# The first down projection in seven block products in place of eight, for three of its four groups

## The chip, the cores and the metric

The kernel runs on one core of one Trainium2 chip. A core has five engines that run side by side: TensorE (PE in the profile, its weight loads PEld), VectorE (DVE), ScalarE (ACT), GpSimd (POOL) and SyncE (SP), which here only starts DMAs. Each engine works through its own instructions in the order written and waits for others on semaphores. The metric is the device time of one execution in microseconds; the lower the better.

## The reference, cut to what matters

Two transformer blocks follow one another on an input of 512 tokens and 1024 features, all in float32. The change touches the feed-forward part of the first block:

```python
x = layer_norm(DEEPNORM_ALPHA * x + mix, ln1_g, ln1_b)            # 512 x 1024
h = jnp.square(jax.nn.relu(jnp.einsum("bsd,df->bsf", x, w_ff1)))  # 512 x 4096
ff = jnp.einsum("bsf,fd->bsd", h, w_ff2)                          # 512 x 1024
x = layer_norm(DEEPNORM_ALPHA * x + ff, ln2_g, ln2_b)
```

Before it stands a block of attention in two branches, after it a second block with a gated delta rule, an attention and a gated feed-forward part. None of these is touched.

## The kernel before, in words

Everything is held feature by token: a tile of 128 partitions holds 128 features, its 512 columns are the tokens. A weight matrix is cut into panels of 128 output features; a panel (`Wraw`, 128x1024) holds eight blocks of 128x128, one for each 128 input features, and is the stationary operand. Float32 products are made of two parts each, a high part (`Whi`, `Rm`, type fp32r) and the rest (`Wlo` and its like): ScalarE copies the raw tile to the high part ("split"), VectorE subtracts it from the raw tile ("low"). One block product is three matmuls of 128x128 by 128x512: low weights by high data, high by low, high by high. A panel is thus 24 matmuls into one PSUM bank (`project`, and the `mm` item of TensorE).

The feed-forward part takes up-panels (`w_ff1`) and down-panels (`w_ff2`) in groups: nine up-panels (0 to 8), eight down-panels over hidden features 0 to 7 (group 0), eight up-panels, group 1, eight, group 2, seven, group 3 (`ff_order`). So one up-panel always runs ahead of its group, except before group 3. After each up-panel comes the item `relu2`: ScalarE's ReLU out of the bank, VectorE's square, ScalarE's copy to the high part, VectorE's low part. After each down-panel comes `down`: VectorE adds the bank onto the residual tile `F(m)` in SBUF; group 0 first scales it by ALPHA in the same instruction. In group 3 sums for the layer norm follow as well.

All engines walk one list, `WORK`, made by `order_of_work`, and each does its own share of each item in that order. An instruction that has to wait therefore holds up all that stand behind it on its engine. `take` keeps four panels split ahead (`HL`) and four raw buffers loading (`RAW`); `low_weights`, called after the fourth block of a panel, puts the pending lows into the list. `Waits` leaves out a wait that a former one covers.

Of the kernel before, what the change touches and what calls it, by code (L numbers as in the profile page):

```python
# [118 lines left out]
NTH = {p: n for n, p in enumerate(PANELS)}  # L119
RAW = 4  # L120
HL = 4
# [21 lines left out]
def order_of_work():  # L143

    work, side, later = [], [], []
    st = {"loads": 0, "splits": 0, "lows": 0, "taken": 0, "done": 0}

# [19 lines left out]
    def ready_weights(upto):  # L167
        while st["splits"] < min(len(PANELS), upto) and st["splits"] - HL < st["done"]:
            while st["loads"] < min(len(PANELS), st["splits"] + RAW):
                load_weights()  # L170
            do("split", st["splits"])
            st["splits"] += 1

    def low_weights(upto=None):
# [13 lines left out]
    def project(name, i, steps=0, flush_at=3, then=None, between=(), low_at=LOW_AT):  # L188
        n = take(name, i)
        many = steps_of(name)  # L190
        do("panel", n)
        for p, k in enumerate(k_order(name)):
            do("mm", n, k)
            if p == many - 1:
                st["done"] = n + 1
            if p == flush_at:
                flush()
            for q, *item in between:
                if q == p:
# [8 lines left out]
        return n  # L208

    def project_first(names, skew=0, between=(), lows=None, apart=False):  # L210
# [223 lines left out]

    first = project_first([("w_ff1", i) for i in range(3)], apart=True)
    for kind, i in FF1:
        if kind == "up":
            n = first[i] if i < 3 else project("w_ff1", i)
            do("relu2", i)
        else:  # L440
            for m in range(8):
                n = project("w_ff2", 8 * i + m)
                do("down", n)
                if i == 3:
                    do("sum", 1, m)

# [312 lines left out]

RING_OF = {"panel": "P", "panelb": "P", "score": "S", "babank": "S", "baturn": "S", "vturn": "T", "turn": "T",  # L760
# [100 lines left out]
SUM1, SUM2, SQ, SUM1_ALL = 22, 23, 24, 27  # L861
RELU, SQUARE = 28, 31
CG, WBA, R1 = 45, 44, 38
KTM, VTM, QTM, GK, GQ = 0, 4, 8, 12, 16
# [5 lines left out]
U3, C3, R2, R3 = 24, 27, 39, 40  # L870
HID = [(2 * j, 2 * j + 1) for j in range(8)] + [(32, 33)]
HID2 = [(16 + 2 * j, 17 + 2 * j) for j in range(9)]
# [35 lines left out]
def build(nc, a, out):  # L908

    ctx = ExitStack()  # L910
    with ctx:
        def sb(name, shape, dt=F32):
            return ctx.enter_context(nc.sbuf_tensor(name, shape, dt))

        Fm = sb("Fm", [128, 49, 512])
        Rm = sb("Rm", [128, 22, 512], F32R)
# [27 lines left out]
        def G(i):  # L944
            return Xf[:, i, :]

        def bank(*item):
# [84 lines left out]


        def features(name, i, k):
            if name == "w_in":
# [9 lines left out]
            if name == "w_ff2":  # L1045
                return tuple(R(j) for j in HID[(8 * (i // 8) + k) % 9])
            if name in ("w_in_2", "w_up"):
# [5 lines left out]
        def parts_of(name, i, k):  # L1053
# [248 lines left out]
        def tensor_engine(e):  # L1302
            w = Waits(e)

            def mm(o, l, r, first=True, last=True):
                return e.matmul(o, l, r, start=first, stop=last)  # L1306

            def tr(o, x):
                return e.transpose(o, x, ident)  # L1309
# [6 lines left out]
            for what, *i in WORK:  # L1316
                if what == "mm":
# [381 lines left out]
        def scalar_engine(e):  # L1699
# [5 lines left out]
            def panel(n):  # L1705
                w.wait_ge(SG["panel"], n + 1)
                return bank("panel", n)

            for what, *i in WORK:
                if what == "split":  # L1710
                    n, = i
                    part = slice(512 if n == 0 else 0, 128 * steps_of(PANELS[n][0]))
                    w.wait_ge(SG[f"landed{n % RAW}"], 16 * (n // RAW + 1))
                    if n >= HL:
                        w.wait_ge(SG["panel"], n - HL + 1)
                    act(Whi[:, n % HL, part], Wraw[:, n % RAW, part]).then_inc(SG["w_hi"], 1)

# [137 lines left out]
                elif what == "splity":  # L1855
                    j, = i
                    w.wait_ge(SG["normed"], at("normed", 0, j))
                    act(R(16 + 2 * j), F(j), ACT.Identity, bias=col("ln1_b", j), scale=col("ln1_g", j)).then_inc(SG["y_hi"], 1)

                elif what == "relu2":  # L1860
                    j, = i
# [3 lines left out]
                    act(F(RELU + j % 3), b, ACT.Relu).then_inc(SG["relu"], 1)  # L1865
                    w.wait_ge(SG["squared"], j + 1)
                    if j >= 9:
                        w.wait_ge(SG["panel"], NTH["w_ff2", 8 * ((j - 9) // 8) + 7] + 1)
                    act(R(HID[j % 9][0]), F(SQUARE + j % 3)).then_inc(SG["hid_hi"], 1)

# [158 lines left out]
                elif what == "gated2":  # L2029
# [5 lines left out]
                    if j >= 9:  # L2035
                        w.wait_ge(SG["panel"], NTH["w_down", 8 * ((j - 9) // 8) + 7] + 1)
                    act(R(HID2[j % 9][0]), F(C3 + g % 6)).then_inc(SG["hid2_hi"], 1)
# [18 lines left out]
        def vector_engine(e):  # L2056
# [20 lines left out]
            def panel(n, item="panel"):  # L2077
                w.wait_ge(SG["panel"], n + 1)
                return bank(item, n)

            for what, *i in WORK:
                if what == "low":
                    n, = i
                    part = slice(512 if n == 0 else 0, 128 * steps_of(PANELS[n][0]))
                    w.wait_ge(SG["w_hi"], n + 1)
# [218 lines left out]
                elif what == "lowy":  # L2304
# [3 lines left out]
                    tt(R(17 + 2 * j), F(j), R(16 + 2 * j).bitcast(F32), ALU.subtract).then_inc(SG["y_lo"], 1)  # L2308

                elif what == "relu2":  # L2310
                    j, = i
                    w.wait_ge(SG["relu"], at("relu2", j))
                    if j >= 3:
                        w.wait_ge(SG["hid_hi"], j - 2)
                    f = F(SQUARE + j % 3)
                    tt(f, F(RELU + j % 3), F(RELU + j % 3), ALU.mult).then_inc(SG["squared"], 1)
                    w.wait_ge(SG["hid_hi"], j + 1)
                    hi, lo = (R(s) for s in HID[j % 9])
                    tt(lo, f, hi.bitcast(F32), ALU.subtract).then_inc(SG["hid_lo"], 1)

                elif what == "down":
                    n, = i
                    g, m = PANELS[n][1] // 8, PANELS[n][1] % 8
                    b = panel(n)
                    if g == 0:
                        w.wait_ge(SG["y_hi"], m + 1)
                        w.wait_ge(SG["y_lo"], m + 1)
                        stt(F(m), F(m), ALPHA, b, ALU.mult, ALU.add).then_inc(SG["down"], 1)
                    else:
                        w.wait_ge(SG["down"], at("down", NTH["w_ff2", 8 * g - 8 + m]))  # L2330
                        tt(F(m), F(m), b, ALU.add).then_inc(SG["down"], 1)

# [425 lines left out]
        def sync_engine(e):  # L2758
# [5 lines left out]
            for what, *i in WORK:  # L2764
                if what == "load":
# [3 lines left out]
                    if n >= RAW:  # L2769
                        w.wait_ge(SG["w_hi"], n - RAW + 1)  # L2770
                        w.wait_ge(*low_part(n - RAW))
                    if n == 0:
                        dma(SG["first_landed"], Wraw[:, 0, 0:512], a[name][j][:, 0:512])
# [40 lines left out]
                elif what == "gdnconsts":  # L2814
                    w.wait_ge(SG["gates_added"], at("merge", 7))
                    for t in range(3):
                        width = min(512, N_G * 128 - 512 * t)
# [115 lines left out]
```

## Time and profile before

| | |
|---|---|
| three runs | 1444.02 us median, 1443.52 to 1445.72 |
| the profiled execution | 1445.06 us, its span 1442.8 us |
| PE busy | 1418.2 us, 98% |
| VectorE busy | 817.0 us, 57% |
| ScalarE busy | 612.7 us, 42% |
| granted TensorE clock over the span | 1.0 |
| group 0 on TensorE | 444.04 to 487.56 us from the span's start |

The difference between the execution and its span is what lies around the first and last instruction, 2.3 us. Busy time of PE is that of overlapping matmuls: one that is recorded with 389 ns is followed by the next after less. The distance between starts is therefore what is read for the pace. VectorE and ScalarE rows too are recorded with a short tail that the next instruction overlaps.

### The profile page before, as it was taken

How to read it: one execution, taken by the hardware profiler on the slowest of the kernel's cores; microseconds unless marked ns; L12 is line 12 of the kernel's file. 1: busy time of each engine (PE TensorE's matmuls, PEld its weight loads, DVE VectorE, ACT ScalarE, POOL GpSimd, SP SyncE). 2: the span in 40 equal slices, each digit the busy share in tenths (PEclk: the TensorE clock that was granted, in tenths of full speed). 3: DMA queues.
4: the chain of work that ended last, by engine and by line, in shares of the span. 5: the costliest groups of instructions: out<-in, count | busy, mean ns of one | idle time of the engine just before them, and what ended most of it. 6: DMA issues, size and time to landing. Idle time of an engine off the chain costs nothing.

```text
span 1442.8 us, 20161 instructions
## 1 busy us (share of the span) xinstructions
PE 1418.2 (98%) x7966; PEld 1136.9 (79%) x7966; DVE 817.0 (57%) x1408; ACT 612.7 (42%) x1113; POOL 124.9 (9%) x119
## 2 busy tenths in 40 slices
PE   8999999999999999999999999999999999999998
PEld 6777777788788888888877777776778888888887
DVE  4545556656674343443468766576555673664464
ACT  4544455632362232322335755345444441442334
POOL 0000000012100000000012000440020110110012
PEclk9999999999999999999999999999999999999999
DMA  7222222123223232233223222110232332233222
GB/s 270 74 70 92 82 87 74 63 74 112 88 88 103 96 99 97 91 101 101 90 104 132 89 73 67 52 47 1 103 103 73 102 116 99 92 102 103 83 67 70
DMA packets 41501, 130.94 MB, mean 91 GB/s; under 512 B 4928, under 2 KB 7360, under 8 KB 41408
## 3 DMA queue, kind: packets, MB, share of 16 engines
q1 hardware_dynamic: 40544, 128.60, 26.5%
q8 instruction: 64, 1.05, 0.3%
q10 hardware_dynamic: 864, 1.05, 0.2%
q14 instruction: 29, 0.24, 0.1%
HBM read 124.92 MB, written 4.19 MB: 89 GB/s over the span
## 4 chain that ended last, share of the span: by engine, by line
PE 93%; DVE 3%; ACT 2%; issue 1%; DMA 1%; POOL 0%; SPq 0%; POOLq 0%; DVEq 0%; ACTq 0%
PE bank L1306 90%; PE bank L1309 3%; ACT Fm L1703 1%; DVE Fm L2061 1%; DVE Fm L2166 1%; DMA Fm<-in_x_dram 0%; DMA Fm<-in_relb_dram 0%; SPq L2762 0%; POOL Fm L2665 0%; DVE Fm L2065 0%; ACT Whi L1703 0%; POOL Xf L2665 0%; DVE sm L2065 0%; ACT Rm L1703 0%; DVE Fm L2069 0%
## 5 line engine op out<-in xcount | busy, mean ns | idle before, releaser
L1306 PE MATMUL bank<-Rm,Whi 128*128 128x512 f32 (+1 forms) x2840 | 874.5, 389 | 9.3 <-ACT Whi L1703 6.0
L1306 PEld LDWEIGHTS bank<-Rm,Whi 128*128 128x128 f32 x2840 | 532.8, 188 | 120.7 <-ACT Whi L1703 6.0
L1306 PE MATMUL bank<-Rm,Wlo 128*128 128x512 f32 (+1 forms) x1420 | 565.4, 398 | 2.0 <-issue 1.8
L2061 DVE TENSOR_TENSOR Wlo<-Wraw,Whi 128x1024 fp32r<-128x1024 f32 (+2 forms) x225 | 283.8, 1265 | 112.5 <-ACT Whi L1703 111.8
L1306 PEld LDWEIGHTS bank<-Rm,Wlo 128*128 128x128 f32 x1420 | 267.6, 188 | 61.4 <-issue 7.5
L1703 ACT ACTIVATE Whi<-Wraw 128x1024 fp32r<-128x1024 f32 (+2 forms) x225 | 232.5, 1038 | 187.1 <-PE bank L1306 181.3
L1306 PE MATMUL bank<-Xr,Whi 128*128 128x512 f32 (+1 forms) x760 | 228.4, 382 | 0.0
L2665 POOL TENSOR_TENSOR Fm<-Fm 128x512 f32<-128x512 f32 (+1 forms) x89 | 102.4, 1157 | 780.0 <-ACT Fm L1703 489.2
L1703 ACT ACTIVATE Fm<-bank 128x512 f32<-128x512 f32 (+4 forms) x200 | 92.4, 482 | 170.7 <-PE bank L1306 106.0
L1306 PEld LDWEIGHTS bank<-Xr,Whi 128*128 128x128 f32 x760 | 141.1, 188 | 27.9
L1306 PE MATMUL bank<-Xr,Wlo 128*128 128x512 f32 (+1 forms) x380 | 145.6, 383 | 0.0
L2061 DVE TENSOR_TENSOR Fm<-Fm,bank 128x512 f32<-128x512 f32 (+2 forms) x130 | 77.7, 621 | 118.0 <-PE bank L1306 117.8
L1703 ACT ACTIVATE Fm<-Fm 128x512 f32<-128x512 f32 (+2 forms) x119 | 61.5, 518 | 96.6 <-DVE Fm L2061 61.3
L1306 PE MATMUL bank<-Fm 128*64 128x128 f32 (+8 forms) x872 | 95.1, 323 | 4.3 <-ACT Fm L1703 1.9
L1703 ACT ACTIVATE Fm<-Fm,par 128x512 f32<-128x512 f32 (+1 forms) x68 | 48.1, 710 | 110.2 <-DVE Fm L2061 110.2
L2061 DVE TENSOR_TENSOR Fm<-Fm 128x512 f32<-128x512 f32 x78 | 53.5, 695 | 61.0 <-ACT Fm L1703 54.6
L1703 ACT ACTIVATE Fm<-Fm,sm 128x512 f32<-128x512 f32 (+3 forms) x93 | 53.5, 578 | 79.1 <-DVE sm L2065 66.4
L1306 PEld LDWEIGHTS bank<-Fm 128*64 128x64 f32 (+4 forms) x872 | 59.2, 155 | 34.5 <-issue 25.3
L1306 PEld LDWEIGHTS bank<-Xr,Wlo 128*128 128x128 f32 x380 | 71.4, 188 | 13.8
L2061 DVE TENSOR_TENSOR Rm<-Fm,Rm 128x512 fp32r<-128x512 f32 x57 | 38.9, 689 | 52.8 <-ACT Rm L1703 52.3
L2069 DVE SCALAR_TENSOR_TENSOR Fm<-Fm,par 128x511 f32<-128x511 f32 x88 | 65.4, 746 | 1.7 <-ACT Fm L1703 0.2
L1703 ACT ACTIVATE Rm<-Fm 128x512 fp32r<-128x512 f32 x54 | 33.7, 631 | 71.1 <-POOL Fm L2665 44.5
(100 smaller groups left out, 716.3 us busy)
## 6 DMA issues: line engine op xcount, KB each, us to landing
Wraw<-in_w_in_dram SPq DMA_DIRECT2D x67, 512.0 KB, 3.3
Wraw<-in_w_ff_dram SPq DMA_DIRECT2D x64, 512.0 KB, 3.2
Wraw<-in_w_up_dram SPq DMA_DIRECT2D x44, 512.0 KB, 3.2
Wraw<-in_w_o_dram SPq DMA_DIRECT2D x16, 512.0 KB, 3.3
Wraw<-in_w_down_dram SPq DMA_DIRECT2D x16, 512.0 KB, 3.2
Wraw<-in_w_ab_dram SPq DMA_DIRECT2D x8, 512.0 KB, 3.2
Wraw<-in_w_down_end_dram SPq DMA_DIRECT2D x8, 384.0 KB, 3.0
Fm<-in_relb_dram SPq DMA_DIRECT2D x8, 256.0 KB, 5.9
```

The source lines that it names most:

```text
L1306: return e.matmul(o, l, r, start=first, stop=last)
L1309: return e.transpose(o, x, ident)
L1703: return e.activation(o, x, func, **kw)
L2061: return e.tensor_tensor(o, x, y, op)
L2069: return e.scalar_tensor_tensor(out=o, in0=x, scalar=s, in1=y, op0=op0, op1=op1)
L2166: e.tensor_tensor_reduce(p, bank("score", u, j)[:, 0:n], strip[:, 512 - n:512], 1.0, LOW, ALU.add, ALU.max, mx).then_inc(SG["masked"], 1)
L2665: return e.tensor_tensor(o, x, y, op)
```

## The change

For groups 0 to 2 the down-panels are taken in pairs n, n+1. A pair, over 1024 hidden features and 512 tokens, is a product of two by two blocks: the stationary side has the halves of panel n (`a11`, `a12`) and of panel n+1 (`a21`, `a22`), each four 128x128 blocks; the moving side has the two halves of the hidden features (even and odd tiles, the weights are reordered to suit on the host, `halves`) by the two halves of the tokens. Seven products of such blocks, with sums of blocks as operands, replace eight. Each `product` is 4 x 3 matmuls of 128x128 by 128x256.

- VectorE sums on the weight side, for each pair (`blocks`): half 0 is `a21 + a22`, then that less `a11`, the second waiting for the first; half 1 is two more. Each is 128x512. ScalarE's `blocksplit` (128x1024) and VectorE's `blocklow` (128x1024) turn each half into high and low part. Panel n+1 is split itself in its second half only.
- On the hidden side (`hidden`), for each two tiles: VectorE makes a sum of 128x512 and two of 128x256, each waiting for the one before, ScalarE makes four high parts (one 128x256, three 128x512) and VectorE four low parts. They replace the two high and two low parts of `relu2`.
- Six `fold` additions of VectorE take the place of two `down` additions: products 1, 5, 6, 3 by 128x256, the bank of 2 and 4 by 128x512, and product 7, which goes to both halves of `F(m+1)`, by 128x512. Product 6 adds onto the bank after fold 1 has read it, 3 after fold 5, 7 after fold 6.
- Banks: a pair uses three (`total`, `single`, `fifth`), the ring P has six.
- The scaling by ALPHA is a ScalarE instruction after each of the first eight up-panels.
- The square (and ReLU) of up-panels 8, 16 and 24 is moved from behind that up-panel to behind fold 5 of the first pair.
- Group 3 stays by panels, its blocks in the order 0, 2, 4, 6, 1, 3, 5, 7. SyncE's load of a panel waits for the block sums of the panel whose buffer it takes, and its load of constants for the second block (`gdnconsts`) waits for the last down-panel.

TensorE's order in each pair is 1, 2, 5, 6, 4, 3, 7; products 5 and 6 need half 0 of the weight sums, 3 and 7 half 1.

```diff
@@ project
             if p == low_at:
                 low_weights()
+                if n + 1 in PAIRS:
+                    sum_parts(2 * st["pairs"] + 1)
...
+    def block_sums(upto):
+        while st["sums"] < min(upto, st["ready"]):
+            do("blocks", PAIRS[st["sums"] // 2], st["sums"] % 2)
+            st["sums"] += 1
+
+    def sum_parts(upto):
+        block_sums(upto)
+        while st["parts"] < min(upto, st["sums"]):
+            do("blocksplit", PAIRS[st["parts"] // 2], st["parts"] % 2)
+            do("blocklow", PAIRS[st["parts"] // 2], st["parts"] % 2)
+            st["parts"] += 1
...
+    def first_seven(name, i, then):
...
+        low_weights(st["taken"])
+        do("product", n, 1)
+        do("fold", n, 1)
+        sum_parts(2 * r + 1)
+        do("product", n, 2)
+        do("product", n, 5)
+        do("fold", n, 5)
+        do(*then)
+        sum_parts(2 * r + 2)
+        do("product", n, 6)
+        do("fold", n, 6)
+        low_weights(st["taken"] + 1)
+        do("product", n, 4)
+        do("fold", n, 4)
+        do("product", n, 3)
+        do("fold", n, 3)
+        low_weights()
+        sum_parts(2 * r + 3)
+        do("product", n, 7)
+        do("fold", n, 7)
+        block_sums(2 * r + 4)
...
+    def seven_products(name, i):
...
+        sum_parts(2 * r + 1)
+        do("product", n, 1)
+        sum_parts(2 * r + 2)
+        low_weights(st["taken"] + 1)
+        do("fold", n, 1)
+        do("product", n, 2)
+        low_weights()
+        block_sums(2 * r + 3)
+        do("product", n, 5)
+        do("fold", n, 5)
+        block_sums(2 * r + 4)
+        do("product", n, 6)
+        do("fold", n, 6)
+        sum_parts(2 * r + 3)
+        do("product", n, 4)
+        do("fold", n, 4)
+        do("product", n, 3)
+        do("fold", n, 3)
+        do("product", n, 7)
+        do("fold", n, 7)
...
     for kind, i in FF1:
         if kind == "up":
             n = first[i] if i < 3 else project("w_ff1", i)
-            do("relu2", i)
+            if i not in (8, 16, 24):
+                do("relu2", i)
+            if i % 2 and i < 24:
+                do("hidden", i // 2)
+            if i < 8:
+                do("alpha", i)
+        elif i < 3:
+            first_seven("w_ff2", 8 * i, ("relu2", 8 * i + 8))
+            for m in range(2, 8, 2):
+                seven_products("w_ff2", 8 * i + m)
...
@@ tensor_engine
+                elif what == "product":
...
+                    for k in range(4):
+                        q = 4 * g + k
+                        w.wait_ge(SG["hid_hi"], moving_made(q, p))
+                        w.wait_ge(SG["hid_lo"], moving_made(q, p))
+                        xh, xl = moving(q, p)
+                        s = slice(128 * k, 128 * k + 128)
+                        add(o, lo[:, s], xh, p in (1, 2, 5) and k == 0)
+                        add(o, hi[:, s], xl)
+                        m = add(o, hi[:, s], xh, False, k == 3)
+                    m.then_inc(SG["product"], 1)
```

## Rows read from the trace of the kernel before

**Rows 1.** The page: busy time and share of each engine, and the chain by engine.
```profile
PE 1418.2 (98%) x7966; PEld 1136.9 (79%) x7966; DVE 817.0 (57%) x1408; ACT 612.7 (42%) x1113; POOL 124.9 (9%) x119
...
PE 93%; DVE 3%; ACT 2%; issue 1%; DMA 1%; POOL 0%; SPq 0%; POOLq 0%; DVEq 0%; ACTq 0%
```

**Rows 2.** Windows on groups 0 to 2: length, each engine's busy us, clock, DMA.
```profile
444.04:487.56 43.52, 43.52 (x193) 36.04 (x192) 15.99 (x17) 9.61 (x10) 0.00 (x0) 1.00 0.33 108
531.00:574.60 43.60, 43.60 (x194) 36.08 (x193) 15.99 (x17) 9.60 (x10) 0.00 (x0) 1.00 0.33 109
618.00:661.60 43.60, 43.60 (x194) 36.12 (x193) 15.99 (x17) 9.60 (x10) 0.00 (x0) 1.00 0.33 109
```

**Rows 3.** Timeline of PE, 512-column matmuls: start, us, engine, line, operation.
```profile
438.15 0.61 PE L1306 MATMUL bank<-Xr,Whi 128*128 128x512 f32 x2
438.60 0.39 PE L1306 MATMUL bank<-Rm,Wlo 128*128 128x512 f32 x1
```

**Rows 4.** Timeline of PE in the last stage, 256-column matmuls; then a window there.
```profile
1418.63 0.28 PE L1306 MATMUL bank<-Rm,Wlo 128*128 128x256 f32 x1
1418.75 0.40 PE L1306 MATMUL bank<-Rm,Whi 128*128 128x256 f32 x2
1418.99 0.28 PE L1306 MATMUL bank<-Rm,Wlo 128*128 128x256 f32 x1
...
1416.00:1428.00 12.00, 12.00 (x103) 12.00 (x102) 4.30 (x9) 9.39 (x21) 6.39 (x7) 1.00 0.00 1
```

**Rows 5.** Timeline of ACT and DVE beside one up-panel, 438 to 443 us.
```profile
438.80 0.60 ACT L1703 ACTIVATE Fm<-bank 128x512 f32<-128x512 f32 x1 [2.50 <-PE bank L1306]
440.16 0.63 ACT L1703 ACTIVATE Rm<-Fm 128x512 fp32r<-128x512 f32 x1 [0.76 <-DVE Fm L2061]
440.69 1.04 ACT L1703 ACTIVATE Whi<-Wraw 128x1024 fp32r<-128x1024 f32 x1
...
439.43 0.69 DVE L2061 TENSOR_TENSOR Fm<-Fm 128x512 f32<-128x512 f32 x1 [1.88 <-ACT Fm L1703]
440.82 0.69 DVE L2061 TENSOR_TENSOR Rm<-Fm,Rm 128x512 fp32r<-128x512 f32 x1 [0.70 <-ACT Rm L1703]
441.77 1.22 DVE L2061 TENSOR_TENSOR Wlo<-Wraw,Whi 128x1024 fp32r<-128x1024 f32 x1 [0.26 <-ACT Whi L1703]
```

**Rows 6.** Timeline of DVE where instructions follow one another without a wait.
```profile
424.37 1.23 DVE L2061 TENSOR_TENSOR Wlo<-Wraw,Whi 128x1024 fp32r<-128x1024 f32 x1 [0.26 <-ACT Whi L1703]
425.51 0.68 DVE L2061 TENSOR_TENSOR Fm<-Fm 128x512 f32<-128x512 f32 x1
...
749.39 2.48 DVE L2061 TENSOR_TENSOR Fm<-Fm,bank 128x512 f32<-128x512 f32 x4 [0.38 <-PE bank L1306]
...
1105.24 0.69 DVE L2061 TENSOR_TENSOR Rm<-Fm,Rm 128x512 fp32r<-128x512 f32 x1 [4.27 <-ACT Rm L1703]
1105.85 1.22 DVE L2061 TENSOR_TENSOR Wlo<-Wraw,Whi 128x1024 fp32r<-128x1024 f32 x1
...
1421.53 0.74 DVE L2061 TENSOR_TENSOR Fm<-Fm,bank 128x256 f32<-128x256 f32 x2
```

**Rows 7.** Timeline of DVE: one instruction that waits for the one before it.
```profile
746.28 0.15 DVE L2279 COPY sm<-bank 128x4 f32<-128x4 f32 x1
746.47 0.16 DVE L2061 TENSOR_TENSOR sm<-sm 128x4 f32<-128x4 f32 x1
```

**Rows 8.** Timeline: a DVE instruction, and the weight load that waited for it.
```profile
761.06 1.67 DVE L2069 SCALAR_TENSOR_TENSOR Rm<-Fm,par,Rm 128x512 fp32r<-128x512 f32 x1
...
762.79 0.53 PEld L1306 LDWEIGHTS bank<-Rm,Whi 128*128 128x128 f32 x3 [0.62 <-DVE Rm L2069]
```

**Rows 9.** Timeline of PE at the kernel's start, and a window there.
```profile
5.99 0.79 PE L1306 MATMUL bank<-Rm,Whi 128*128 128x512 f32 x1 [5.99 <-ACT Whi L1703]
...
8.24 1.05 PE L1306 MATMUL bank<-Rm,Whi 128*128 128x512 f32 x2
...
9.52 1.05 PE L1306 MATMUL bank<-Rm,Whi 128*128 128x512 f32 x2
...
11.65 0.45 PE L1306 MATMUL bank<-Rm,Wlo 128*128 128x512 f32 x1
...
5.00:10.00 5.00, 4.00 (x9) 2.84 (x10) 4.30 (x7) 4.34 (x8) 0.00 (x0) 1.00 1.04 400
```

**Rows 10.** Waits of PE over the whole span: us in total, times, longest.
```profile
PE bank L1306 <- ACT Fm L1703: 2.5, 5, 0.7
...
PE bank L1306 <- DVE Fm L2061: 1.4, 2, 1.2
```

**Rows 11.** Timeline of SP after the last loads of the stage.
```profile
736.83 1.37 SPq L2762 DMA_DIRECT2D Fm<-in_cg_dram  x3
...
752.35 14.68 SPq L2762 DMA_DIRECT2D x_scratch<-Fm  x7
```

More of the change, by code:

```diff
@@ L119, with doubled, pair_of, product_end @@
 NTH = {p: n for n, p in enumerate(PANELS)}
+def doubled(n):
+    name, i = PANELS[n]
+    return name == "w_ff2" and i < 24
+PAIRS = [n for n, (_, i) in enumerate(PANELS) if doubled(n) and i % 2 == 0]
+PAIR_NO = {n: r for r, n in enumerate(PAIRS)}
+def pair_of(n):
+    return n - PANELS[n][1] % 2 if doubled(n) else None
+PRODUCTS = (1, 2, 5, 6, 4, 3, 7)
+def product_end(n, p):
+    return 7 * PAIR_NO[n] + PRODUCTS.index(p) + 1
+HALF_ORDER = (0, 2, 4, 6, 1, 3, 5, 7)
 RAW = 4
@@ L145, in order_of_work @@
     work, side, later = [], [], []
-    st = {"loads": 0, "splits": 0, "lows": 0, "taken": 0, "done": 0}
+    st = {"loads": 0, "splits": 0, "lows": 0, "taken": 0, "done": 0, "sums": 0, "ready": 0, "parts": 0, "pairs": 0}
     def do(*item):
@@ L208, in project @@
         return n
+    def first_seven(name, i, then):
+        n = take(name, i)
+        take(name, i + 1)
+        r = st["pairs"]
+        for bank in ("total", "single", "fifth"):
+            do(bank, n)
+        low_weights(st["taken"])
[19 more added lines that the diff above has]
+        block_sums(2 * r + 4)
+        st["pairs"] += 1
+        st["done"] = n + 2
+    def seven_products(name, i):
+        n = take(name, i)
+        take(name, i + 1)
+        r = st["pairs"]
+        for bank in ("total", "single", "fifth"):
+            do(bank, n)
+        sum_parts(2 * r + 1)
[18 more added lines that the diff above has]
+        do("fold", n, 7)
+        st["pairs"] += 1
+        st["done"] = n + 2
     def project_first(names, skew=0, between=(), lows=None, apart=False):
@@ L1084, in low_part, with finished @@
             return SG["w_lo"], at("low", n)
+        def finished(n):
+            if pair_of(n) is not None:
+                return SG["product"], product_end(pair_of(n), 2 if pair_of(n) == n else 4)
+            return SG["panel"], n + 1 - sum(2 for m in PAIRS if m < n)
         def emptied(n):
@@ L1129, in let_go @@
             kind, i = item[0], item[1:]
+            if kind in ("total", "single", "fifth"):
+                return [(SG["fold"], fold_end(*i, {"total": 7, "single": 4, "fifth": 3}[kind]))]
             if kind == "panel":
@@ L1306, in mm, with add @@
                 return e.matmul(o, l, r, start=first, stop=last)
+            def add(o, l, r, first=False, last=False):
+                return e.matmul(o, l, r, start=first, stop=last, skip_group_check=True)
             def tr(o, x):
@@ L1858, in scalar_engine @@
                     act(R(16 + 2 * j), F(j), ACT.Identity, bias=col("ln1_b", j), scale=col("ln1_g", j)).then_inc(SG["y_hi"], 1)
+                elif what == "blocksplit":
+                    n, half_ = i
+                    r = PAIR_NO[n]
+                    w.wait_ge(SG["blocks"], 4 * r + 2 * half_ + 2)
+                    if r > 0:
+                        w.wait_ge(SG["product"], product_end(PAIRS[r - 1], 7 if half_ else 6))
+                    hi, _, raw = combined(half_)
+                    act(hi, raw).then_inc(SG["block_hi"], 1)
                 elif what == "relu2":
@@ L2083, in vector_engine @@
                     n, = i
[L2084 removed]
+                    part = slice(512 if n == 0 or pair_of(n) == n - 1 else 0, 128 * steps_of(PANELS[n][0]))
                     w.wait_ge(SG["w_hi"], n + 1)
@@ L2771, in sync_engine @@
                         w.wait_ge(*low_part(n - RAW))
+                        if pair_of(n - RAW) is not None:
+                            w.wait_ge(SG["blocks"], 4 * PAIR_NO[pair_of(n - RAW)] + 4)
                     if n == 0:
```

209 lines of the change are left out of this document (174 added, 35 removed).

## The prediction, before the changed kernel was run

> **What bounds the kernel now.** I read the page first: PE is busy for 98% of the span and makes 93% of the chain that ended last [rows 1]; the reader is to see that nothing else bounds the whole. Then the windows on the three groups that change: PE is busy for all of each 43.5 us, VectorE for 16.0, ScalarE for 9.6, GpSimd for nothing [rows 2]. So a matmul saved is time saved, as long as the others keep up, and VectorE has 27.5 us to spare in a group. Last the timelines, for the pace of each kind of instruction and for what one takes to release another.
>
> **What TensorE saves.** With 512 columns a block product (three matmuls) starts each 0.68 us: the Xr matmuls at 438.15 and the next Wlo matmul at 438.60 are 0.45 apart, for two, and the third is as long [rows 3]; eight blocks make 5.44 us, a group of eight panels 43.52. With 256 columns three start each 0.36 us (1418.63 to 1418.99), weight loads included, at clock 1.00 [rows 4]. So a product of 4 x 3 matmuls takes 1.44 us, seven take 10.08, where two panels took 10.88: 0.80 us saved a pair, 9.6 in twelve. The ratio is 0.93 and not 7/8, as the halved matmul takes 0.12 and not 0.113. The Trainium skill, "TensorE: Matmul & The Clock Gate", section "Back-to-back issue gap", gives an isolated gap of N/2.4 plus 2.5 ns: 109 ns at 256 columns and 216 at 512, by which 48 of the one less 84 of the other would save 1.19 us a pair, an estimate of 14 in all; the trace disagrees with 120 and 227 ns, and is what I go by.
>
> **What VectorE gets.** Steps between starts where nothing waits: 1.14 us for 128x1024, 0.61 for 128x512 (1105.24 to 1105.85), 0.60 out of a bank (2.48 less 0.68, over three), 0.33 for 128x256 out of a bank (0.74 less 0.41) [rows 6]. In a pair it had two lows and two additions, 3.5 us. Now: three of 1024 columns (low of panel n, two `blocklow`), five of 512 (four sums, the half low of panel n+1), folds of 4 x 0.33 and 2 x 0.60: 3.42 + 3.05 + 2.52 = 9.0 us, against TensorE's 10.08. It fits, but barely, so the order and the handovers decide. Handovers: matmul pace to consumer 0.20 us (panel ends at 438.60, ReLU at 438.80), ScalarE to VectorE and back 0.03 (ReLU ends 439.40, square 439.43) [rows 3, 5]; an own result 0.04 after the recorded end [rows 7]; VectorE to weight load 0.06 [rows 8]. A handover counts the full recorded duration: 0.69 for 512 columns, 1.23 for 1024, ScalarE 1.05 for 1024, 0.60 for the ReLU.
>
> **The queue, walked.** T = 0 is the end of up-panel 8, when product 1 of a group's first pair can start. Without waits its product 5 is due at 2.88, product 3 at 7.20.
>
> *Stall A, before product 5.* Up-panel 7 ends at -5.44. ReLU -5.24 to -4.64, square to -3.92, sum of 512 -3.88 to -3.19, the two dependent ones of 256 start at -3.15 and -2.69, four lows at -2.36, -2.03, -1.42 and -0.81. Only then the weight low of up-panel 8's turn: it waits for a split that stands behind ALPHA on ScalarE, and starts at -0.07. First weight sum 1.07, the dependent one 1.80 to 2.49, ScalarE 2.53 to 3.58, `blocklow` 3.61 to 4.84, product 5 at 4.90: 2.02 us late. In groups 1 and 2, without ALPHA, 1.89.
>
> *Stall B, before product 3.* Product 5 ends at 6.34, fold 5 starts 6.54, the moved square 6.87, two sums 7.48 and 8.09 to 8.78, ScalarE to 9.87, `blocklow` 9.90 to 11.13, product 3 at 11.19. Products 6 and 4 ended at 9.22: 1.97 us late. In group 2 the moved item also makes the high and low part of tile 24, a handover (0.03 + 0.63 + 0.03) and a low: 1.39 more, 3.36.
>
> *Stall C, second pair.* Product 3 ends at 12.63, 7 at 14.07. Fold 3 12.83, half low 13.16, sums 13.77 and 14.50 to 15.19, ScalarE to 16.28, `blocklow` 16.31 to 17.54, product 5 at 17.60, due at 16.95: 0.65.
>
> *Stall D, second pair.* VectorE is behind now: fold 7 of the first pair 17.45, sums 18.05 and 18.66 to 19.35, ScalarE 19.39 to 20.44, `blocklow` 20.47, weight low 21.61, and only then fold 1, 22.75 to 23.17, though product 1 had ended at 15.51. Product 6 adds onto that bank, so it starts at 23.23 instead of 19.04: 4.19 us.
>
> Pairs three and four run at 10.08: in the third, fold 1 comes just before its product 6. Sum by group: stalls 8.83, 8.70 and 10.09 us, 27.6 together, against 9.6 saved: **18.0 us slower**. Some 9 us of VectorE work in a group stood within its former slack, but in the first two pairs it comes too late.
>
> Bounds. The walk's weak points are VectorE's pace on these operands and the own-result handover; neither sum nor fold with a broadcast bank stands in the trace as such. With all VectorE durations 10% shorter (it then gains 0.06 us on each sum, as if a 512 sum went at 0.55), the same walk gives +12.3; 10% longer, +23.9. With an own result at 0.10 and TensorE's restart at 0.19, a whole recorded weight load, +20.1. I take the rows as they stand, since form and size are theirs.
>
> **Costed at nothing.** ALPHA and the split hidden parts on ScalarE: 0.5 us and 0.4 more a panel where it worked 2.3 of 5.44 [rows 5]; cover gone, they push back the split, which is the 0.13 in stall A. The hidden lows in the up-panels: VectorE then works 6.9 of 10.88 us for two panels, by the steps above. Half a split saved on ScalarE. The loads' new wait: in the second pair the sums end at 19.35, a load lands some 4 later, and that panel's split is due near 29. Behind it on SP stand only more loads. The constants are issued at 736.83 and would now follow the last panel, 6.4 us later; behind them stand the spill stores, 752.35 [rows 11], and they land before. ALPHA leaving the addition, the new order of blocks in group 3: the same lengths; tile 30 is wanted fourth, 2.0 us in, but its parts were made beside up-panel 31.
>
> **Against the runs.** The trace's execution took 1445.06 us, its span 1442.8; the median of the runs is 1.0 lower. The difference goes onto the median: 1444.0 + 18.0 = 1462.
>
> **Rivals.**
> 1. *VectorE keeps up; faster.* All its work hides, TensorE takes 9.6 us less: 1434.4. For it: 9.0 us of work in 10.08, 27.5 us of slack in a group [rows 2]. Against: the slack is of the group, the stalls are of its first two pairs, and each is a chain of named instructions. It decides where stalls in a group fall below 3.2 us; a fifth less on each VectorE duration would not do that, only another order on its queue than I read. 0.12.
> 2. *Half of it.* Stall D does not come, because pair one's tail is shorter than walked (fold 7 and the sums of the next pair reach ScalarE sooner), the rest does: 27.6 - 12.6 - 9.6 = +5.4, 1449. 0.08.
> 3. *The clock falls too.* At the start, after 5.99 us of nothing, matmuls run 0.43 apart (8.24 to 9.52 for three), the 1.2 GHz pace, until about 11.65, though the column shows 1.00 [rows 9]. The longest later wait of PE is 1.2 us [rows 10], so no row tells what 4.19 do. If it fell, 256 columns take 0.213 in place of 0.12 over 5.6 us: 2.4 lost, of which 0.6 is taken up before product 7; 1.8 to 2.4 for each of three D stalls: +24, 1468. The Trainium skill, "TensorE: Matmul & The Clock Gate", section "Why this matters for your kernels", warns of idle gaps in TensorE that send it back to half rate. 0.15.
>
> My own case has 0.65. The range holds it with its bounds, rival 3 and most of rival 2: 1449 to 1471. Outside are rival 1 and the far tails, near 0.18. By 0.2%, 2.9 us, which is about what a measurement of this kernel can tell from no change: faster 0.13, within 0.03, slower 0.84.
>
> **What would show it.** PE starts 0.12 apart in products and 10.08 us for pairs three and four of a group. In the first pair a PE wait near 2 us on VectorE before product 5 and before product 3, in the second one near 4 before product 6, released by a 128x256 addition. VectorE near 100% busy over the second pair, and ScalarE's 1024-column parts starting right behind VectorE's sums. PE busy down by the saving, its waits up by some 28 us. I am wrong if the second pairs show no wait over 1 us, if three 256-column matmuls take other than 0.36, or if the waits stand in the up-panels.

## The result, and the profile after

The changed kernel takes 1475.57 us in the median of six runs (1471.43 to 1476.77), the one before 1443.94 beside it: the ratio is 1.0212, with an interval from 1.0201 to 1.0223. It is 31.6 us slower where 18.0 were forecast, and outside the range of 1449 to 1471.

The page of the changed kernel: span, busy time by engine, the chain by engine and by line. L1488 is the matmul of a `product`, L1485 that of a panel, L2299 VectorE's two-input operations, L1914 ScalarE's.

```profile
span 1474.5 us, 21350 instructions
PE 1425.6 (97%) x8398; PEld 1163.3 (79%) x8398; DVE 910.1 (62%) x1588; ACT 646.6 (44%) x1169; POOL 124.3 (8%) x119
...
PE 89%; DVE 5%; ACT 3%; issue 2%; POOL 0%; DMA 0%; POOLq 0%; DVEq 0%; ACTq 0%
PE bank L1485 79%; PE bank L1488 7%; PE bank L1491 3%; DVE Fm L2299 3%; ACT Fm L1914 1%; ACT Er L1914 1%; DVE Wlo L2299 1%; DVE Fm L2404 0%; DMA Fm<-in_x_dram 0%; DVE Er L2299 0%; ACT Whi L1914 0%; POOL Fm L2970 0%; POOL Xf L2970 0%; ACT Rm L1914 0%; DVE Fm L2303 0%
```

PE makes 89% of the chain where it made 93% [rows 1]; VectorE has 5% for 3, ScalarE 3% for 2, and time without a releaser 2% for 1. Its windows, by stage (length, busy us of PE, PEld, DVE, ACT and POOL, granted clock, DMA share, GB/s): the three groups, what follows to the layer norm, on to the second block's reload, and the rest.

```profile
443.37:495.38 52.01, 44.21 (x337) 43.44 (x337) 38.01 (x56) 16.54 (x18) 0.00 (x0) 0.93 0.29 102
538.90:590.72 51.82, 44.24 (x338) 43.48 (x337) 37.85 (x56) 16.54 (x18) 0.00 (x0) 0.93 0.30 102
634.24:688.84 54.60, 46.29 (x338) 45.70 (x337) 38.74 (x57) 17.17 (x19) 0.00 (x0) 0.87 0.28 97
688.84:770.60 81.76, 81.76 (x364) 67.73 (x363) 40.28 (x44) 26.33 (x35) 8.39 (x7) 1.00 0.29 97
770.60:1055.60 285.00, 274.13 (x2610) 206.85 (x2609) 200.51 (x421) 151.33 (x371) 45.38 (x46) 0.99 0.19 65
1055.60:1474.50 418.90, 412.32 (x1910) 343.86 (x1910) 235.55 (x312) 156.87 (x221) 45.79 (x39) 1.00 0.29 96
```

Beside [rows 2] a group is 52.0, 51.8 and 54.6 us long instead of 43.5: 27.9 more in all. VectorE works 38 us in one instead of 16. PE is idle for 8 us of each, and the clock column, 1.00 before, has 0.93 and 0.87. Outside the groups one stretch is longer, 285.0 against 280.7 us; it is called the later stretch below. The other two are as they were (81.8 and 418.9, before 81.6 and 418.9).

The waits of PE in groups, in the timeline of group 0 (start, us, engine, line, operation, what it waited for). Product 1 starts at 443.41.

```profile
448.31 0.95 PE L1488 MATMUL bank<-Rm,Er 128*128 128x256 f32 x6 [1.87 <-issue]
454.69 2.19 PE L1488 MATMUL bank<-Rm,Er 128*128 128x256 f32 x9 [1.84 <-issue]
462.35 0.95 PE L1488 MATMUL bank<-Rm,Er 128*128 128x256 f32 x6 [0.19 <-issue]
467.92 1.27 PE L1488 MATMUL bank<-Rm,Er 128*128 128x256 f32 x6 [3.90 <-DVE Fm L2299]
```

These are the four places of the walk: products 5 and 3 of the first pair, 5 and 6 of the second. The profile names VectorE for the last alone and puts the others down to issue. For the first two the times show the same engine: the weight load comes 0.06 us after the end of a `blocklow`.

```profile
446.99 1.23 DVE L2299 TENSOR_TENSOR Er<-Fm,Er 128x1024 fp32r<-128x1024 f32 x1 [1.12 <-ACT Er L1914]
448.28 0.77 PEld L1488 LDWEIGHTS bank<-Rm,Er 128*128 128x128 f32 x6 [2.04 <-issue]
...
453.36 1.23 DVE L2299 TENSOR_TENSOR Er<-Fm,Er 128x1024 fp32r<-128x1024 f32 x1 [1.13 <-ACT Er L1914]
454.65 0.86 PEld L1488 LDWEIGHTS bank<-Rm,Er 128*128 128x128 f32 x4 [2.01 <-issue]
```

VectorE's timeline before the last wait:

```profile
461.03 1.23 DVE L2299 TENSOR_TENSOR Er<-Fm,Er 128x1024 fp32r<-128x1024 f32 x1 [1.12 <-ACT Er L1914]
462.17 0.68 DVE L2299 TENSOR_TENSOR Fm<-Fm,bank 128x512 f32<-128x512 f32 x1
462.77 0.69 DVE L2299 TENSOR_TENSOR Fm<-Wraw 128x512 f32<-128x512 f32 x1
463.37 0.69 DVE L2299 TENSOR_TENSOR Fm<-Wraw,Fm 128x512 f32<-128x512 f32 x1
465.18 1.22 DVE L2299 TENSOR_TENSOR Er<-Fm,Er 128x1024 fp32r<-128x1024 f32 x1 [1.12 <-ACT Er L1914]
466.32 1.22 DVE L2299 TENSOR_TENSOR Wlo<-Wraw,Whi 128x1024 fp32r<-128x1024 f32 x1
467.46 0.41 DVE L2299 TENSOR_TENSOR Fm<-Fm,bank 128x256 f32<-128x256 f32 x1
```

Fold 7, two sums, a handover to ScalarE and back, `blocklow`, a low, and then the 0.41 us of fold 1 for which PE stands at 467.46. Last the clock, in windows of 2 us over that group (columns as above):

```profile
452.00:454.00 2.00, 0.85 (x8) 0.64 (x6) 0.87 (x2) 1.06 (x1) 0.00 (x0) 1.00 0.35 94
454.00:456.00 2.00, 1.31 (x6) 1.34 (x7) 1.51 (x3) 0.00 (x0) 0.00 (x0) 0.69 1.00 399
456.00:458.00 2.00, 2.00 (x12) 2.00 (x11) 0.45 (x2) 0.00 (x0) 0.00 (x0) 0.50 0.11 39
458.00:460.00 2.00, 2.00 (x18) 2.00 (x18) 1.87 (x3) 0.06 (x1) 0.00 (x0) 0.96 0.00 0
...
466.00:468.00 2.00, 0.08 (x1) 0.08 (x1) 2.00 (x4) 0.00 (x0) 0.00 (x0) 1.00 0.99 389
468.00:470.00 2.00, 2.00 (x11) 2.00 (x12) 1.97 (x4) 0.00 (x0) 0.00 (x0) 0.60 0.02 8
470.00:472.00 2.00, 2.00 (x12) 2.00 (x11) 2.00 (x5) 1.43 (x2) 0.00 (x0) 0.54 0.02 4
472.00:474.00 2.00, 2.00 (x19) 2.00 (x18) 1.48 (x2) 1.21 (x2) 0.00 (x0) 1.00 0.77 244
```

The reader is to see PE's busy time and the clock (the third figure from the end) together: PE idles, starts again, and then the clock falls to 0.50, which is 1.2 GHz of 2.4; 12 matmuls in 2 us where 18 or 19 run as the clock comes back. In group 2 it falls about 1 us before the wait of 3.23 us is over:

```profile
644.00:645.90 1.90, 0.00 (x0) 0.00 (x0) 0.78 (x2) 1.06 (x1) 0.00 (x0) 1.00 0.24 37
645.90:646.90 1.00, 0.00 (x1) 0.03 (x1) 1.00 (x2) 0.00 (x0) 0.00 (x0) 0.51 0.92 360
646.90:650.00 3.10, 3.10 (x14) 3.10 (x15) 0.99 (x3) 0.00 (x0) 0.00 (x0) 0.50 0.49 200
```

### The profile page after: what moved, and what is told of

Same layout as the page of the kernel before. It is cut to its first block, busy times and chain, and to the rows that moved or that the text cites. A ratio compares the mean times of both kernels' runs of the same rounds, so it can differ in the third digit from the quotient of the medians.

```text
span 1474.5 us, 21350 instructions
## 1 busy us (share of the span) xinstructions
PE 1425.6 (97%) x8398; PEld 1163.3 (79%) x8398; DVE 910.1 (62%) x1588; ACT 646.6 (44%) x1169; POOL 124.3 (8%) x119
## 3 DMA queue, kind: packets, MB, share of 16 engines
HBM read 124.92 MB, written 4.19 MB: 88 GB/s over the span
## 4 chain that ended last, share of the span: by engine, by line
PE 89%; DVE 5%; ACT 3%; issue 2%; POOL 0%; DMA 0%; POOLq 0%; DVEq 0%; ACTq 0%
PE bank L1485 79%; PE bank L1488 7%; PE bank L1491 3%; DVE Fm L2299 3%; ACT Fm L1914 1%; ACT Er L1914 1%; DVE Wlo L2299 1%; DVE Fm L2404 0%; DMA Fm<-in_x_dram 0%; DVE Er L2299 0%; ACT Whi L1914 0%; POOL Fm L2970 0%; POOL Xf L2970 0%; ACT Rm L1914 0%; DVE Fm L2303 0%
## 5 line engine op out<-in xcount | busy, mean ns | idle before, releaser
L1485 PE MATMUL bank<-Rm,Whi 128*128 128x512 f32 (+1 forms) x2488 | 766.6, 389 | 10.3 <-ACT Whi L1914 5.8
L1485 PEld LDWEIGHTS bank<-Rm,Whi 128*128 128x128 f32 x2488 | 467.1, 189 | 107.5 <-issue 5.9
L1485 PE MATMUL bank<-Rm,Wlo 128*128 128x512 f32 (+1 forms) x1244 | 497.5, 400 | 1.1 <-issue 0.9
L2299 DVE TENSOR_TENSOR Wlo<-Wraw,Whi 128x1024 fp32r<-128x1024 f32 (+2 forms) x225 | 277.5, 1238 | 96.4 <-ACT Whi L1914 95.5
L1485 PEld LDWEIGHTS bank<-Rm,Wlo 128*128 128x128 f32 x1244 | 234.7, 189 | 54.6 <-issue 7.5
L1914 ACT ACTIVATE Whi<-Wraw 128x1024 fp32r<-128x1024 f32 (+2 forms) x225 | 226.5, 1014 | 103.3 <-PE bank L1485 81.6
L1485 PE MATMUL bank<-Xr,Whi 128*128 128x512 f32 (+1 forms) x712 | 213.7, 382 | 0.0
L1914 ACT ACTIVATE Fm<-bank 128x512 f32<-128x512 f32 (+4 forms) x200 | 92.3, 482 | 171.0 <-PE bank L1485 105.3
L2299 DVE TENSOR_TENSOR Fm<-Fm,bank 128x256 f32<-128x256 f32 (+2 forms) x186 | 102.7, 571 | 100.8 <-PE bank L1485 73.8
L1485 PEld LDWEIGHTS bank<-Xr,Whi 128*128 128x128 f32 x712 | 132.1, 188 | 25.8
L1485 PE MATMUL bank<-Xr,Wlo 128*128 128x512 f32 (+1 forms) x356 | 136.3, 383 | 0.0
L1914 ACT ACTIVATE Fm<-Fm 128x512 f32<-128x512 f32 (+2 forms) x127 | 66.4, 524 | 96.0 <-DVE Fm L2299 61.3
L2299 DVE TENSOR_TENSOR Fm<-Fm 128x512 f32<-128x512 f32 (+1 forms) x114 | 71.9, 638 | 53.3 <-ACT Fm L1914 45.7
L1485 PE MATMUL bank<-Fm 128*64 128x128 f32 (+8 forms) x872 | 95.6, 324 | 3.1 <-DVE Fm L2299 1.2
L1914 ACT ACTIVATE Fm<-Fm,par 128x512 f32<-128x512 f32 (+1 forms) x68 | 48.1, 710 | 110.2 <-DVE Fm L2299 110.2
L1914 ACT ACTIVATE Fm<-Fm,sm 128x512 f32<-128x512 f32 (+3 forms) x93 | 53.5, 578 | 77.8 <-DVE sm L2303 65.1
L1485 PEld LDWEIGHTS bank<-Fm 128*64 128x64 f32 (+4 forms) x872 | 59.2, 155 | 33.6 <-issue 25.4
L1485 PEld LDWEIGHTS bank<-Xr,Wlo 128*128 128x128 f32 x356 | 66.9, 188 | 13.0
L1914 ACT ACTIVATE Er<-Fm 128x1024 fp32r<-128x1024 f32 (+2 forms) x43 | 36.1, 840 | 92.2 <-DVE Fm L2299 64.2
L1488 PE MATMUL bank<-Rm,Er 128*128 128x256 f32 x324 | 53.1, 308 | 23.7 <-issue 12.5
L1488 PEld LDWEIGHTS bank<-Rm,Er 128*128 128x128 f32 x324 | 47.4, 213 | 25.7 <-issue 13.9
```

Source lines behind the costliest of these rows:

```text
L1488: return e.matmul(o, l, r, start=first, stop=last, skip_group_check=True)
L1914: return e.activation(o, x, func, **kw)
L2299: return e.tensor_tensor(o, x, y, op)
```

## The experiments

Theory Q+C: VectorE's queue makes TensorE wait where the walk says (Q), and TensorE's clock falls after such waits (C). Rivals: P, the products themselves bring the clock down; V, VectorE has too much work wherever it stands. Each set of the e-runs ran beside the kernel before, at 1444.5 to 1444.9 us.

**e1: the waits filled.** The new item issues matmuls on operands already there into an unread bank.

```diff
+        do("spare", n, 2, 14)
         do("product", n, 5)
...
+        do("spare", n, 4, 14)
         do("product", n, 3)
... (seven_products)
+        if i % 8 == 2:
+            do("spare", n, 5, 32)
         do("product", n, 6)
```

> The changed kernel with spare matmuls on TensorE in the four places where it stood waiting: 14 of 128x256 before product 5 and 14 before product 3 of a group's first pair, 32 before product 6 of the second, on operands that are already there, into a bank nobody reads. They last less (1.7, 1.7 and 3.8 us) than the waits of 2.0, 2.0 and 4.1 us. Theory Q+C (queue and clock): VectorE comes as late as before, so the 18 us of waits less the saving stay, but TensorE's clock does not fall; 1444 + 18 = 1462, granted clock 1.00 in the three groups. Rival P (the half-rate stretches come from the products themselves, as more weight loads for each column, and not from standing still): they stay, 1475 or more. Rival V (VectorE is later than I walked and the clock column is only a symptom): within 2 us of 1475.6.

1465.11 us (1464.55 to 1467.78), ratio 1.0143 (1.0128 to 1.0158). The windows of its groups:

```profile
443.50:492.90 49.40, 48.44 (x397) 47.68 (x397) 37.85 (x56) 16.44 (x18) 0.00 (x0) 1.00 0.31 107
536.40:585.70 49.30, 48.48 (x398) 47.71 (x397) 37.78 (x56) 16.44 (x18) 0.00 (x0) 1.00 0.30 108
629.20:679.90 50.70, 48.47 (x398) 47.70 (x397) 38.48 (x57) 17.07 (x19) 0.00 (x0) 1.00 0.31 105
```

Clock 1.00 with more matmuls than ever in the stage: P falls; in the groups the standing still was the cause. 149.3 us in three groups, against 130.6 before: the queue alone costs 18.8, where the walk gave 18.0. The clock's share is 158.4 less 149.3, 9.1 us in the traces' groups. The medians are 10.5 apart, but the later stretch differs too, 283.0 us in e1's trace against 285.0. That stretch, 2.3 us longer than before, is the largest part of why the whole came out at 1465 and not 1462; the queue's 0.8 us and the kernel before, 0.9 us slower beside this set, add to it.

**e2: stall B alone.** `sum_parts(2 * r + 2)` in `first_seven` moved from behind the square to behind fold 1.

> One move: in a group's first pair the second half of the weight sums with its split and low stands behind fold 1 in place of behind fold 5 and the moved square. Theory Q+C: stall B goes (2.0, 2.0 and 3.4 us, of which 0.8 comes back in group 2 before product 7), so 6.3 us less of waiting, and the half-rate stretch that follows stall B in each group goes too, up to 1.7 us for each 3.4 us of it: 1464 to 1468. Stall D stays with its half-rate stretches. Rival Q alone (the clock falls by D alone): 1469.3. Rival P: 1469 to 1471 with as many half-rate stretches as in the changed kernel.

1466.17 us (1463.94 to 1467.81), ratio 1.0146 (1.0131 to 1.0161), as Q+C has it; no wait stands before product 3 any more, those before products 5 and 6 stay (1.87 and 3.91 us in group 0).

**e3: fold 1 first.**

```diff
         do("product", n, 1)
+        do("fold", n, 1)
         sum_parts(2 * r + 2)
         low_weights(st["taken"] + 1)
-        do("fold", n, 1)
```

> One move: in pairs two to four of a group fold 1 stands right behind product 1, ahead of the low of the second half and the next panel's low. Theory Q+C: stall D before product 6 shrinks from 4.2 to 0.7 us, but product 3 now waits 2.6 for the second half's low, so only 0.8 us a group goes, 2.5 in all; the single wait of 4 us goes too and with it perhaps one half-rate stretch a group: 1468 to 1473. Who thinks that the order of that one addition is the whole cost of stall D expects 4.2 us a group less, 1463.

1465.05 us (1461.75 to 1466.36), ratio 1.0142 (1.0125 to 1.0159): better than I expected of it, though the queue does as walked. PE's waits in the second pair are 0.42 before product 6 and 2.37 before product 3, instead of one of 3.90. In the traces the three groups take 9.3 us less than the changed kernel's 158.4. The queue accounts for 2.5 of them by the walk; the other 6.8 go with the clock, which is 0.97, 1.00 and 0.97 by group in place of 0.93, 0.93 and 0.87. The medians are 10.5 apart, but e3's later stretch is also 5.8 us shorter than the changed kernel's. One wait here, the 3.23 us before product 3 of group 2, left the clock at 1.00; in the changed kernel the clock fell in the same wait.

**e9 and e10: the spare matmuls in halves**, before the long wait alone, and before the short ones alone.

> The changed kernel with the 32 spare matmuls before product 6 of the second pair alone. All spare ones together kept the clock and brought 10.5 us. If what I now hold is right, that half-rate stretches follow the waits of 2 us as well as those of 4, this brings about half: those behind the long waits (three stretches, 3.4 to 6.8 us, at most half of each lost, less 0.6 us of slack), 4 to 6 us: 1470. The view of my prediction, that only the long waits let the clock fall, gives all of it: 1465.

> The other half: 14 spare matmuls before product 5 and 14 before product 3 of a group's first pair, none before the long wait. By what I now hold the stretches behind product 3 go and those behind the long wait stay: 4 to 6 us less than the changed kernel, 1470. If only the long waits counted: 1475.6, no change.

e9 took 1465.46 us (ratio 1.0147, 1.0133 to 1.0160), e10 1473.31 (1.0198, 1.0182 to 1.0214). My expectation of an even split was wrong: most of the clock's cost follows the waits of 3.9 us. In the traces e9's three groups take 151.2 us, e10's 155.6, with all filled 149.3: 6.3 us for three long waits left open, 1.8 for six short ones. At each of the eleven waits of 3.9 us (two in the changed kernel, three each in e2, e7 and e10) the clock fell, at the earliest 1.6 us before the wait's end and at the latest 1.3 after it. Behind the short ones it fell in some groups and not in others: 0.97 and 1.00 in e9's groups 0 and 1, whose waits were alike (1.87 and 1.84, 1.75 and 1.84). What decides for a wait of 2 or 3 us stays open.

**e7: the moved square put back.** `relu2` for 8, 16 and 24 behind their own up-panel.

> The changed kernel with the ReLU and square of up-panels 8, 16 and 24 back behind their up-panel. The queue gives 2.7 us less waiting: stall B falls from 2.0 to 1.4 in two groups and from 3.4 to 1.9 in the third, as the square no longer stands between fold 5 and the sums. Theory Q+C: 1472.9, and perhaps a half-rate stretch fewer, down to 1469. Who holds the move for a gain expects over 1477.

1470.44 us (1466.97 to 1472.64), ratio 1.0176 (1.0161 to 1.0192). So this part of the change costs 5 us by itself. In the traces 3.4 of them lie in the groups (155.0 us), where the waits before product 3 are 1.24, 0.71 and 0.65 in place of 1.84, 1.84 and 3.23; 1.8 lie in the later stretch (283.2 us), which the square doesn't touch. The clock gained nothing: 0.93, 0.90 and 0.90 by group, for 0.93, 0.93 and 0.87.

**e4: the same work, earlier and even.** In `project`, and `first_seven` in the order of `seven_products`, with the square behind fold 5:

```diff
-                if n + 1 in PAIRS:
+                if n + 2 in PAIRS:
                     sum_parts(2 * st["pairs"] + 1)
+                if n + 1 in PAIRS:
+                    sum_parts(2 * st["pairs"] + 2)
```

> The weight sums of a group's first pair start one up-panel earlier (half 0 beside up-panel 7, half 1 beside up-panel 8) and the first pair uses the even order of the later pairs: next pair's sums behind products 2 and 5 in place of the end. The work is the same. Theory Q+C: VectorE has room there; waits left are 0.8 us before product 6 and 0.1 before 7, 1.5 in group 2, 3.9 in all against 9.6 saved, and no clock falls in the groups: 1444 - 5.7 = 1438.3. Rival P (half rate by the products themselves): ten us more, 1448. Rival V (VectorE has too much work wherever it stands, 9 of 10 us a pair): waits of 1 us or more in every pair, 1448 to 1460.

1442.10 us (1438.10 to 1443.78), ratio 0.9979 (0.9970 to 0.9988). Its groups:

```profile
443.50:485.25 41.75, 40.65 (x337) 40.38 (x336) 35.52 (x54) 15.80 (x18) 0.00 (x0) 1.00 0.38 127
528.80:569.90 41.10, 40.62 (x337) 40.36 (x336) 34.94 (x53) 15.39 (x17) 0.00 (x0) 1.00 0.36 129
613.40:655.90 42.50, 40.82 (x338) 40.37 (x337) 35.68 (x54) 15.90 (x18) 0.00 (x0) 1.00 0.37 125
```

125.4 us, 5.2 less than before, where the walk had 5.7. V falls: VectorE is busy for 35 of 42 us and still hardly anyone waits. All that the change lost in the groups, waits and clock, it lost by the order in which VectorE was asked. The median is 3.8 us above the walk, and not by these groups; 0.9 of it is the kernel before, slower beside this set. **e8** has the square behind fold 6, and is otherwise the same.

> The early and even order of the fourth experiment with the moved square behind fold 6. The walk gives 0.4 us less waiting than there: 1441.7 against its 1442.1, so the same within the noise. It is here for a second look at the same schedule: whether the three groups again take some 125.4 us with granted clock 1.00, and where, if anywhere, the clock falls after them.

1442.14 us, ratio 0.9977 (0.9967 to 0.9987), groups 41.7, 41.1 and 42.4.

**e5 and e6: the weight sums on GpSimd**, in the order of the change (e5) and of e4 (e6, and e11 once more): the `blocks` item moved from `vector_engine` to `pool_engine`.

> The changed kernel with the four weight sums of each pair on GpSimd, which does nothing in this stage, in place of VectorE; order of the list as it was. VectorE's share of a pair falls from 9.0 to 6.6 us, and the sums no longer stand behind folds. Theory Q+C: by the same walk only 1.3 us of waiting are left (product 3 in group 2), so 1444.9 - 8.3 = 1436.6 if the two engines do not slow each other; in the trace of the kernel before both took longer side by side (a low of 1024 columns 1.48 to 2.05 us in place of 1.23), and with VectorE a fifth slower I get waits of 5 to 10 us: 1437 to 1446. Who holds that TensorE itself is the cause (half rate by 256-column products) expects over 1455; who holds that the loads or the banks are late expects no change from 1475.6.

> The early and even order of the fourth experiment, with the weight sums on GpSimd. The walk has no wait left, 1444.9 - 9.6 = 1435.3; with the slowing of VectorE beside GpSimd 1436 to 1441. If the 3.8 us by which the fourth experiment's median missed its walk come from later stages and not from the three groups, they show here too: 1439.

> The kernel of the sixth experiment once more, against the one before in more rounds: 1438 to 1441, ratio 0.995 to 0.998, and the three groups in 123.5 us again; the spread of its runs from places after them.

e5: 1447.72 us, ratio 1.0029 (1.0019 to 1.0039), 28 us better than the change, 1.7 outside my range. The waits in its groups are 6.6 us, inside the 5 to 10 that I took for the two engines slowing each other. What I had left out is the clock, which fell behind two waits of 1.85 us (0.96 in groups 0 and 2), and the later stretch, 283.2 us. e6: 1439.83, ratio 0.9969 (0.9955 to 0.9982); e11: 1441.00, 0.9971 (0.9962 to 0.9979). These are the fastest of all; e4 and e8 too are faster than the kernel before, by 0.2%. Groups of e6, and its GpSimd and VectorE in the second of them by form:

```profile
443.00:485.85 42.85, 40.80 (x337) 40.38 (x337) 34.12 (x45) 18.01 (x21) 17.14 (x11) 1.00 0.28 101
529.40:569.70 40.30, 40.30 (x337) 40.26 (x337) 30.03 (x40) 14.88 (x17) 16.02 (x10) 1.00 0.31 106
613.20:653.50 40.30, 40.30 (x337) 40.26 (x336) 30.65 (x41) 15.46 (x18) 16.03 (x10) 1.00 0.31 105
```

```profile
L2953 POOL TENSOR_TENSOR Fm<-Wraw 128x512 f32<-128x512 f32 x5 | 8.3, 1663 | 14.8 <-DVE Er L2301 14.8
...
L2301 DVE TENSOR_TENSOR Wlo<-Wraw,Whi 128x1024 fp32r<-128x1024 f32 x5 | 6.1, 1220 | 0.0
L2301 DVE TENSOR_TENSOR Wlo<-Wraw,Whi 128x512 fp32r<-128x512 f32 x3 | 4.6, 1528 | 0.0
```

Two groups run at 40.3 us, four times the 10.08 of the forecast: TensorE waits for nothing. VectorE's half low takes 1.53 us beside GpSimd, 0.69 without.

**b1 to b7: the untouched stretch.** From the layer norm to the reload (the later stretch) the twelve traces of changed kernels have 279.3 to 286.3 us, 283.2 in the median; only one trace of the kernel before was there. Four more of it:

> The kernel before, unchanged. If the untouched stretch from the layer norm to the reload varies by itself, four looks at it spread over some 279 to 286 us, as the eleven variants did, around 283. If its lengthening belongs to the change, they stay at 280 to 281.

> As for the first look at the kernel before: 279 to 286 us in the untouched stretch if it varies by itself, 280 to 281 if the change lengthens it.

> As for the first look at the kernel before: 279 to 286 us in the untouched stretch if it varies by itself, 280 to 281 if the change lengthens it.

> As for the first look at the kernel before: 279 to 286 us in the untouched stretch if it varies by itself, 280 to 281 if the change lengthens it.

280.9, 280.3, 280.4 and 280.1 us. So the lengthening belongs to the changed kernels, though no instruction of the stretch is another, and in them it varies from run to run: e6 and e11 are one kernel, with 281.4 and 286.3 us. In each trace of the kernel before TensorE waits there once for 0.63 to 0.90 us for nothing the profile shows, at the same matmul; in e4's trace it does not, and in e8's, whose stretch takes 285.8, it does so twice, elsewhere:

```profile
939.53 0.63 PE L1487 MATMUL bank<-Rm,Whi 128*128 128x512 f32 x2 [2.37 <-issue]
957.67 0.34 PE L1487 MATMUL bank<-Xf,Fm 64*64 64x64 f32 x5 [2.12 <-issue]
```

The next three put spare matmuls of 128x256 into the down-panels of the kernel before, behind the first block of each: 18 each for b5 and b6, 9 for b7.

> The kernel before with 18 spare matmuls of 128x256 in each down-panel of groups 0 to 2, 432 in all, as many as the change adds, into a bank nobody reads; some 52 us longer for it. If the number of TensorE instructions ahead moves its waits for nothing in the later stretch, that stretch leaves 280.1 to 280.9 us, to 282 to 286, with issue waits over 1.5 us. If only what the change does to the other engines or to its tiles matters, it stays at 280 to 281 with one issue wait of 0.6.

> The same once more: with the number of instructions as the cause 279 to 286 us in the untouched stretch, another value than in the first look being no surprise; without it 280 to 281.

> Half as many spare matmuls, 9 in each of the 24 down-panels, some 26 us longer. With the number of instructions as the cause the later stretch leaves 280 to 281 us too, and its issue waits stand at yet other places; without it 280 to 281.

279.9, 281.6 and 282.1 us, with waits for nothing at other matmuls than before: 0.69 in b5, 0.68 and 0.38 in b6, 1.82 in b7. The number of TensorE instructions ahead moves these waits, but not by as much as 432 of them come with in the changed kernels (up to 286.3). The cause of their size stays open.

The waits are not all of it: the clock falls in this stretch too. In the trace of the changed kernel it falls to 0.50 at 775.6 and at 1038.5 us, in e11 behind both waits for nothing, and once each in e2, e7, e8 and e10; of the five traces of the kernel before in b1 alone. Two lines for the changed kernel:

```profile
776.00:779.00 3.00, 3.00 (x9) 1.54 (x8) 1.82 (x4) 0.76 (x2) 0.00 (x0) 0.50 0.00 1
1039.00:1041.00 2.00, 2.00 (x7) 1.42 (x7) 1.62 (x7) 1.18 (x4) 0.00 (x0) 0.50 0.00 0
```

PE is busy there for 274.1 us in place of 270.9, though its matmuls are the same, and idle for 10.9 in place of 9.8. So some 3.3 us of what the stretch grew by in this trace are matmuls at half rate, and 1 us is waiting.

## Why the prediction was wrong, step by step

- **The saving.** Right. Three 256-column matmuls start each 0.36 us, and e6 shows four pairs in 40.30.
- **The walk.** Right in place and size. In group 0 product 5 started 4.90 us after product 1 (forecast 4.90), product 3 at 11.28 (11.19), and the wait before product 6 was 3.90 by the profile, 4.1 from its turn (4.19). Before the second pair's product 5 it was 0.19, not 0.65: product 3 had run at half clock and come late itself. Group 2's wait before product 3 was 3.23 by the profile, 3.46 from its turn (3.36), the moved item's share as forecast. With the clock held the queue costs 18.8 us (18.0). Two of its signs did not come as told: the profile names VectorE for the long wait alone, and PE's busy time went up by 7.4 us (1418.2 to 1425.6) and not down by the saving, as matmuls at half rate last longer.
- **The failed step: "My own case has 0.65"**, with the clock standing through waits of 4 us. I had no row for such a wait but one, 5.99 us at the start with the pace halved behind it [rows 9], and held the absence of a row between 1.2 and 6 us for a reason to let it stand. The near end of a gap in the rows was taken, where the far end was the only one that spoke. The Trainium skill, "TensorE: Matmul & The Clock Gate", section "Why this matters for your kernels", warned of just this; the trace agrees, with 0.50 at every wait of 3.9 us. It should have been the likeliest case. In the groups the fall of the clock cost 9.1 us (e1), the largest part of the 13.6 by which the forecast missed.
- **Rival 3** named it, but at 6 us. Three long waits cost 6.3 in the traces, 2.1 each, inside its 1.8 to 2.4. It had nothing for the short waits and for both together (9.1 in all in the traces' groups), nor for the later stretch.
- **The later stretch.** Costed at nothing without a word, as nothing in it changes. It took 4.4 us more in this trace, some 2.5 in the median of twelve, by waits for nothing and by the clock; what sets them off there is not shown. Groups 18.8 + 9.1, stretch 4.4, less 0.7 that lies ahead of group 0: 31.6.
- **Rivals 1 and 2.** Stall D came, and e4 shows what rival 1 asked for: another order on VectorE's queue.
- **Things at nothing.** The constants' later load and the loads' new wait left no trace: no wait of PE on a DMA or a split in the groups. ALPHA shows as forecast in stall A, 1.87 us in group 0 against 1.75 in the others (0.13 forecast).

## What to carry to other kernels

When work moves from a full engine to one with slack, count the slack where the work stands in the queue, and not over the stage: 9 of 10 us a pair fitted, and the first two pairs still lost 9 us a group. Walk the receiving queue with the rows' durations; it came out to a few tenths. And price a new wait of TensorE at its length and what the clock takes after it; where it can't be avoided, matmuls that nobody reads are cheaper than standing still (e1: 9.1 us back in the groups).

## What the runs showed of the hardware

- A wait of 3.9 us on TensorE brought the 1.2 GHz level every time (eleven waits in four kernels), one of about 2 us in some groups only, one of 3.23 us in the changed kernel but not in e3; a long wait filled with matmuls never (six in e1 and e9).
- The level can be there before the wait is over: 1.0 us before its end in group 2, 1.4 in e10's group 0.
- A fall without a long wait: at 775.6 us in the changed kernel and 747.8 in b1 no wait in the 5 us before is over 0.2 us. The same matmuls in b2 to b4 ran at 1.00.
- The column for the clock showed 1.00 at the kernel's start while matmuls ran 0.43 us apart [rows 9].
- Runs of one kernel spread over 1438.1 to 1443.8 us (e4), where the kernel before spreads over 1443.5 to 1445.9. Two traces of one kernel (e6 and e11) have spans of 1435.6 and 1440.3 us and groups of 123.5 us in both; the later stretch, 281.4 and 286.3, has the whole difference: waits for nothing of 1.8 us in one, 3.5 in the other, and in e11 the clock at 0.50 behind each.
